# Sixteen attention units in a new order, and an output projection out of rounded operands

## The reference, cut to what matters

```
o_c = compressed attention, o_s = selected blocks, o_w = sliding window      # 8 heads, 2 KV heads, head_dim 64
g = sigmoid(gl)
o_att = g[0] * o_c + g[1] * o_s + g[2] * o_w
mixed = concat([rmsnorm(o_lru, out_norm_lru), rmsnorm(o_att, out_norm_att)]) @ w_out
x = x + gt1 * mixed
```

## Time and profile before

| | us |
|---|---|
| median of three runs | 1754.97 |
| lowest, highest | 1753.71, 1760.32 |
| profiled execution, own time | 1750.48 |
| its span | 1748.8 |
| TensorE busy in the span | 1681.2 (96%) |
| VectorE busy | 1298.6 (74%) |
| ScalarE busy | 668.0 (38%) |
| GpSimd busy | 375.2 (21%) |

### The profile page before, as it was taken

One profiled execution on the slowest core, in us unless ns is written; L12 is line 12 of the kernel. 1 busy time (PEld: TensorE's weight loads), 2 busy tenths in 40 slices (PEclk: granted clock), 3 DMA queues, 4 the chain that ended last, 5 costly groups with the idle time before them and its releaser, 6 DMA issues.

```text
span 1748.8 us, 30656 instructions
## 1 busy us (share of the span) xinstructions
PE 1681.2 (96%) x11657; PEld 1567.4 (90%) x11657; DVE 1298.6 (74%) x2673; ACT 668.0 (38%) x1048; POOL 375.2 (21%) x369
## 2 busy tenths in 40 slices
PE   7999997789899999999999999999999999999997
PEld 5699965458799999999899999999999999999997
DVE  0445546751677799998999999948878787878786
ACT  1336524740422233444344444443333333333332
POOL 3211000000000002111454445422322222222220
PEclk9999986999899999999999999999999999999998
DMA  9787676000623147766899999999999999999991
GB/s 342 271 272 273 213 213 242 1 1 1 242 82 99 63 134 275 245 225 210 297 384 383 388 371 390 385 373 387 402 373 337 347 343 345 346 342 351 339 319 63
DMA packets 178038, 466.43 MB, mean 267 GB/s; under 512 B 20399, under 2 KB 92335, under 8 KB 176251
## 3 DMA queue, kind: packets, MB, share of 16 engines
q1 hardware_dynamic: 130298, 289.53, 46.7%
q0 software_dynamic: 44880, 172.82, 26.9%
q10 hardware_dynamic: 2736, 2.49, 0.5%
HBM read 408.21 MB, written 63.37 MB: 270 GB/s over the span
## 4 chain that ended last, share of the span: by engine, by line
PE 86%; DVE 7%; DMA 3%; ACT 2%; issue 1%; ACTq 1%; POOL 0%; DVEq 0%
PE ps L1119 31%; PE ps L1005 26%; PE ps L735 10%; PE ps L957 3%; PE ps L1098 2%; PE ps L640 2%; ACT arena L1162 2%; PE ps L613 1%; PE ps L933 1%; PE ps L925 1%; DVE arena L1697 1%; DVE ul L1832 1%; PE ps L862 1%; PE ps L1014 1%; DMA gw<-stage 1%
## 5 line engine op out<-in xcount | busy, mean ns | idle before, releaser
L1832 DVE TENSOR_TENSOR ul<-raw,uh 128x1024 fp32r<-128x1024 f32 x256 | 311.5, 1222 | 109.8 <-ACT uh L1162 108.2
L1005 PE MATMUL ps<-hh,uh 128*128 128x392 f32 x1024 | 357.4, 349 | 1.6 <-DVE ul L1832 1.6
L1005 PE MATMUL ps<-hl,uh 128*128 128x392 f32 x1024 | 349.0, 341 | 0.0
L1005 PE MATMUL ps<-hh,ul 128*128 128x392 f32 x1024 | 348.6, 340 | 0.0
L1119 PE MATMUL ps<-ah,ul 128*128 128x392 f32 x1000 | 341.9, 342 | 0.0
L1119 PE MATMUL ps<-al,uh 128*128 128x392 f32 x1000 | 341.0, 341 | 0.0
L1119 PE MATMUL ps<-ah,uh 128*128 128x392 f32 x1000 | 339.7, 340 | 0.6 <-DVE al L2055 0.6
L1162 ACT ACTIVATE uh<-raw 128x1024 fp32r<-128x1024 f32 x256 | 270.0, 1056 | 103.3 <-PE ps L1119 89.5
L545 POOL DMA_INDIRECT xT<-in_u,gidx x128 | 177.5, 1387 | 545.1 <-DVE zg L1880 330.2
L545 POOL DMA_INDIRECT xT<-in_v,gidx x128 | 138.1, 1079 | 377.0 <-DVE vacc L2069 359.3
L1162 ACT ACTIVATE zbuf<-ps 128x392 f32<-128x392 f32 x128 | 63.7, 498 | 359.9 <-PE ps L1005 359.8
(11 more groups left out here) (371 smaller groups left out, 2279.4 us busy)
## 6 DMA issues: line engine op xcount, KB each, us to landing
raw<-in_uT SPq DMA_DIRECT2D x128, 512.0 KB, 5.6
raw<-in_v SPq DMA_DIRECT2D x128, 512.0 KB, 6.4
gw<-stage POOLq DMA_DIRECT2D x28, 896.0 KB, 10.8
gr<-gw SPq DMA_DIRECT2D x32, 784.0 KB, 8.3
zs<-zbuf SPq DMA_DIRECT2D x124, 196.0 KB, 5.7
zin<-zs SPq DMA_DIRECT2D x124, 196.0 KB, 5.9
arena<-in_ada_w SPq DMA_DIRECT2D x32, 512.0 KB, 4.3
arena<-in_w_in SPq DMA_DIRECT2D x18, 512.0 KB, 6.3
```

Source lines behind the costliest of these rows:

```text
L1005: last = mm(ps[:, bank, 0:DN], w[x][:, k * P:(k + 1) * P], m[:, k, G0:TOK], start=(k == 0 and x == 0 and m is hh), stop=(k == KD - 1 and x ...
L1832: tt(ul[:, i % 4, :], raw[:, i % 4, :], uh[:, i % 4, :].bitcast(F32), SUB).then_inc(S["lo_done"], 1)
```

## The change

In the attention, the three loops get a new order:

- TensorE: `scores(u + 1)`, then, block by block, the transpositions of unit u (`turn`) and one block of products of unit u - 1 (`apply`). `ptb` has eight blocks in place of four, so two units' turned blocks can stand side by side.
- ScalarE: the exponentials of u + 1 before the scalings of u.
- VectorE: `ttr(u + 1)` before `scale(u)`; the outputs of a query block are moved one unit later.

The output projection is made from rounded operands: ScalarE makes the high parts of the weights (`high_wo`, one per chunk of 128 columns) and of the input (`m_hi`), VectorE the low parts in the place of the originals (`low_wo`, `m_lo`), and TensorE makes three products in place of one fp32 product. Squares of the attention half go to another place, and the counts of some semaphores shift (`WQ_0`, `HQ_0`).

```diff
@@ buffers
+        with nc.sbuf_tensor("m_lo", [P, KD, TOK], F32R) as m_lo:
...
+        with (nc.sbuf_tensor("m_gap", [P, 9360], F32), nc.sbuf_tensor("m_hi", [P, KD, TOK], F32R) as m_hi,
...
-        ptb = at(13520, 4, GRP * P)
+        ptb = at(13520, 8, GRP * P)
@@ TensorE
+            first_turn = [sum(i + 1 for i, _, _ in units[:u]) for u in range(16)]
+
+            def turn(u, kb):
+                if kb == 0:
+                    pe.wait_ge(S["u_p"], GRP * (u + 1))
+                n = first_turn[u] + kb
+                if n >= 2:
+                    pe.wait_ge(S["u_tdone"], n - 1)
+                for r in range(GRP):
+                    last = pe.transpose(ps[:, 4 + n % 2, r * P:(r + 1) * P],
+                                        pbuf[:, (u % 2) * GRP + r, kb * P:(kb + 1) * P], ident[:, :])
+                last.then_inc(S["u_t"], 1)
...
+            def apply(u, kb):
                 i, br, w = units[u]
-                pe.wait_ge(S["u_p"], GRP * (u + 1))
...
+                if kb == 0 and u % 4 == 0 and i >= 2:
+                    pe.wait_ge(S["o_done"], i - 1)
+                if kb == 0 and br == 0:
+                    cached(i, w)
+                pe.wait_ge(S["u_tdone"], first_turn[u] + kb + 1)
+                pt = ptb[:, (u % 2) * 4 + kb, :].rearrange("p (r g q) -> p r g q", g=2, q=P)
+                for g in range(2):
+                    last = mm(ps[half(g), 6 + i % 2, 2 * w * P:2 * (w + 1) * P], vn[:, br * 4 + kb, half(g)], pt[:, :, g, :],
+                              start=False, stop=(br == 1 and kb == i))
+                if kb == i:
+                    last.then_inc(S["u_pv"], 1)
 
             pe.wait_ge(S["pc_tdone"], 4)
...
+            for u in range(17):
+                if u < 15:
+                    scores(u + 1)
+                for kb in range(4):
+                    if u < 16 and kb <= units[u][0]:
+                        turn(u, kb)
+                    if u >= 1 and kb <= units[u - 1][0]:
+                        apply(u - 1, kb)
 
             def project(c, ks):
+                pe.wait_ge(S["wql_done"], WO_0 + c + 1)
+                w = (wo_hi(c), wo_lo[:, :, c * P:(c + 1) * P])
                 for k in ks:
-                    for h in range(2):
-                        last = mm(ps[:, 2 + 2 * (c % 3) + h, 0:HALF], wout[:, k, c * P:(c + 1) * P],
-                                  zT[:, k, h * HALF:(h + 1) * HALF], start=(k == 0), stop=(k == KD - 1))
+                    if c == 0:
+                        pe.wait_ge(S["hl_ready"], MX_0 + max(1, k - 2))
+                    for x, m in ((0, m_hi), (0, m_lo), (1, m_hi)):
+                        for h in range(2):
+                            last = mm(ps[:, 2 + 2 * (c % 3) + h, 0:HALF], w[x][:, k, :], m[:, k, h * HALF:(h + 1) * HALF],
+                                      start=(k == 0 and x == 0 and m is m_hi), stop=(k == KD - 1 and x == 1))
...
-            pe.wait_ge(S["mix_ready"], 1)
@@ ScalarE
-            for u, (i, br, g) in enumerate(units):
-                nk = (i + 1) * P
+            def exps(u):
+                nk = (units[u][0] + 1) * P
                 act.wait_ge(S["u_max"], u + 1)
                 for r in range(GRP):
                     fn(pbuf[:, (u % 2) * GRP + r, 0:nk], pbuf[:, (u % 2) * GRP + r, 0:nk], ACT.Exp,
                        bias=pst(u, 1)[:, r:r + 1], accum_out=pst(u, 2)[:, r:r + 1]).then_inc(S["u_exp"], 1)
+            exps(0)
+            for u in range(16):
+                if u < 15:
+                    exps(u + 1)
+                nk = (units[u][0] + 1) * P
                 act.wait_ge(S["u_exp"], GRP * (u + 1))
                 act.wait_ge(S["u_rs"], u + 1)
                 for r in range(GRP):
                     fn(pbuf[:, (u % 2) * GRP + r, 0:nk], pbuf[:, (u % 2) * GRP + r, 0:nk], ACT.Copy,
                        scale=pst(u, 3)[:, r:r + 1]).then_inc(S["u_p"], 1)
+
+            def high_wo(c):
+                fn(wo_hi(c), wout[:, :, c * P:(c + 1) * P], ACT.Copy).then_inc(S["rounded"], 1)
+            act.wait_ge(S["wout_loaded"], 16)
+            high_wo(0)
+            act.wait_ge(S["lru_dve"], 6)
+            act.wait_ge(S["u_pv"], 12)
+            fn(m_hi[:, 0:4, :], zT[:, 0:4, :], ACT.Copy).then_inc(S["hh_ready"], 1)
+            high_wo(1)
+            high_wo(2)
             act.wait_ge(S["o_done"], 4)
-            fn(hT[:, 0:4, :], zT[:, 4:8, :], ACT.Square).then_inc(S["mix_sq"], 1)
+            fn(x1sq[:, 0:4, :], zT[:, 4:8, :], ACT.Square).then_inc(S["mix_sq"], 1)
             root(3, roots)
+            for c in range(4):
+                act.wait_ge(S["mix_ready"], c + 1)
+                fn(m_hi[:, 4 + c, :], zT[:, 4 + c, :], ACT.Copy).then_inc(S["hh_ready"], 1)
+            high_wo(3)
             for k in range(KD):
                 act.wait_ge(S["proj_ready"], k + 1)
                 fn(x1sq[:, k, :], xT[:, k, :], ACT.Square).then_inc(S["chunk_sq"], 1)
+                if k + 4 < KD:
+                    high_wo(k + 4)
@@ VectorE
+            def low_wo(c):
+                dve.wait_ge(S["rounded"], WO_0 + c + 1)
+                cols = slice(c * P, (c + 1) * P)
+                tt(wo_lo[:, :, cols], wout[:, :, cols], wo_hi(c).bitcast(F32), SUB).then_inc(S["wql_done"], 1)
...
-                    if u >= 1:
-                        dve.wait_ge(S["u_pv"], u)
-                    cp(ptb[:, kb, :], ps[:, 4 + (tcount[0] - 1) % 2, 0:512]).then_inc(S["u_tdone"], 1)
+                    if u >= 2:
+                        dve.wait_ge(S["u_pv"], u - 1)
+                    cp(ptb[:, (u % 2) * 4 + kb, :], ps[:, 4 + (tcount[0] - 1) % 2, 0:512]).then_inc(S["u_tdone"], 1)
...
-            for i in range(4):
-                for q in range(4):
-                    u = 4 * i + q
-                    scale(u)
-                    if u < 15:
-                        ttr(u + 1)
-                    evac(u)
+            def out_moved(i):
                 dve.wait_ge(S["u_pv"], 4 * i + 4)
                 link(cp(zT[:, 4:8, i * P:(i + 1) * P], ps[:, 6 + i % 2, 0:512].rearrange("p (r q) -> p r q", q=P)))
                 dve.sem_inc(S["o_done"], 1)
+            for u in range(16):
+                if u < 15:
+                    ttr(u + 1)
+                scale(u)
+                evac(u)
+                if u and u % 4 == 0:
+                    out_moved(u // 4 - 1)
+            low_wo(0)
+            dve.wait_ge(S["hh_ready"], MX_0 + 1)
+            tt(m_lo[:, 0:4, :], zT[:, 0:4, :], m_hi[:, 0:4, :].bitcast(F32), SUB).then_inc(S["hl_ready"], 1)
+            out_moved(3)
+            for c in (1, 2):
+                low_wo(c)
...
+            for c in range(4):
+                stt(zT[:, 4 + c, 0:SEQ], zT[:, 4 + c, 0:SEQ], par[:, NAG + c:NAG + c + 1], ps[:, 1, :], MUL, MUL).then_inc(S["mix_ready"], 1)
+            for c in range(4):
+                dve.wait_ge(S["hh_ready"], MX_0 + 2 + c)
+                tt(m_lo[:, 4 + c, :], zT[:, 4 + c, :], m_hi[:, 4 + c, :].bitcast(F32), SUB).then_inc(S["hl_ready"], 1)
+            low_wo(3)
...
                 dve.sem_inc(S["proj_ready"], 1)
+                if c + 4 < KD:
+                    low_wo(c + 4)
```

More of the change, by code:

```diff
@@ L67 @@
 KEPT = 4
+WO_0, MX_0 = ZC - 1, KD
+WQ_0, HQ_0 = WO_0 + KD, MX_0 + 5
 ADA_HEAD, ADA_ALL = 4, 36
@@ L125, in build @@
               nc.sbuf_tensor("wl0", [P, KD, P], F32R) as wl0):
+            pass
+        with nc.sbuf_tensor("m_lo", [P, KD, TOK], F32R) as m_lo:
+            pass
+        with (nc.sbuf_tensor("m_gap", [P, 9360], F32), nc.sbuf_tensor("m_hi", [P, KD, TOK], F32R) as m_hi,
+              nc.sbuf_tensor("wo_gap", [P, 17680 - 13520], F32), nc.sbuf_tensor("wo_pages0", [P, 8, 256], F32R) as wo_pages0,
+              nc.sbuf_tensor("wo_pages1", [P, 8, 256], F32R) as wo_pages1, nc.sbuf_tensor("wo_pages2", [P, 8, 256], F32R) as wo_pages2,
+              nc.sbuf_tensor("wo_pages3", [P, 8, 256], F32R) as wo_pages3, nc.sbuf_tensor("wo_lo", [P, KD, D], F32R) as wo_lo):
             pass
@@ L302, in heads, with wo_hi @@
             return [(2 * w + j // 2, j % 2) for j in range(GRP)]
+        def wo_hi(c):
+            return (wo_pages0, wo_pages1, wo_pages2, wo_pages3)[c % 4][:, :, P:2 * P]
         def load_w1(engine, c, s):
@@ L912, in _ @@
                 turn_cached(i)
-            tcount = [0]
-            def apply(u):
-                i, br, w = units[u]
-                pe.wait_ge(S["u_p"], GRP * (u + 1))
[L919 to L935, removed]
@@ L937, in _ @@
-            pe.wait_ge(S["pc_tdone"], 4)
-            for i in range(4):
-                for q in range(4):
-                    u = 4 * i + q
-                    if u < 15:
[L942 to L950, removed]
+            first_turn = [sum(i + 1 for i, _, _ in units[:u]) for u in range(16)]
@@ new lines, in cached @@
+            def cached(i, w):
+                cols = slice(2 * w * P, 2 * (w + 1) * P)
+                for g in range(2):
+                    mm(ps[half(g), 6 + i % 2, cols], vc[0:NCMP_P, 8, half(g)],
```

(26 more changed lines are left out.)

## The result

| | before | changed |
|---|---|---|
| median, us | 1755.26 (4 runs) | 1846.40 (4 runs) |
| lowest, highest | 1753.71, 1760.32 | 1843.09, 1850.21 |
| profiled execution, own time | 1750.48 | 1847.32 |
| its span | 1748.8 | 1845.6 |

The changed kernel takes 1.0516 times as long (95% interval 1.0483 to 1.0549): 91 us more. It was forecast slower, at 1831 in a range of 1798 to 1857.

What follows compares the result with a forecast made beforehand. TensorE's chain was taken to bound the kernel (86% of waits), with attention bound by hand-overs and the projection by columns. Ring +59, clock +28, projection -11 gave +76 on 1754.97: 1831 us, range 1798 to 1857.

Steps and rivals of the forecast that it cites:

- The ring: Attention: scores, sums, exponentials of u+1, normalisation, transposes of u, then scores of u+2 run strictly one after another; +59 us.
- the other side, faster: Rival, attention: scores run a turn ahead of the transposes, the ring stays open and ScalarE bounds; 1721 us, chance 0.03.
- The ring's size at the high clock: Attention: the ring's added time if the clock stays high, +59 us; a 512-key unit 13.2 us against 7.71.
- 40 blocks at 0.43 + 0.47: 36.0: Attention, TensorE's part of the ring: 40 blocks, each 0.43 us for a transposition and 0.47 for a product.
- The interpolated starts: Attention: scores start to exponentials start, units 1 to 15, middle sizes interpolated between 2.12 and 4.04 us; 47 us in all.
- The clock: Attention: TensorE's pauses drop its clock, units 0 to 7 all low, later bursts' first two pairs low; +28 us.
- clock rival: Either of two: the attention's clock stays high (1803 us, chance 0.16) or stays low throughout (1854 us, chance 0.20).
- The projection: Output projection: 384 records of rounded operands, 46.2 us in place of 58.2, with +1 of stall; -11 us.
- the seams: Projection: two new waits at the seam, for the strip sums' root and chunk 4's low part; +1 us, bounds 0 and 5.
- The low parts ahead of the outputs' move: Attention's end: VectorE makes low parts of first weights (1.22 us) and four input chunks (estimated 2.5) before moving outputs.
- a projection that waits for low parts: Listed sign, in the profile after, that the prediction would be wrong; no size given.
- The cover for the other low parts: Projection: VectorE needs 4.4 us a chunk within TensorE's 5.8, so low parts cost nothing; uncovered, four chunks 1.2 late each.

Runs made afterwards that it cites:

- e2: The kernel before with only ScalarE's swap, exponentials of u+1 ahead of the normalisation of u: 1836.3 us, ratio 1.0456.
- e6: The kernel before with TensorE's interleaving and VectorE's sums ahead of the scale, ScalarE in its old order, fp32 projection: 1820.0 us, ratio 1.0367.
- e5: The changed kernel with TensorE's pause in each turn filled by transpositions of the identity that no result uses: 1813.7 us, ratio 1.0321 against the kernel before.
- e8: The kernel before with the rounded projection alone, its first rounding moved into ScalarE's and VectorE's pauses in the last units: 1746.4 us, ratio 0.9934.
- e3: The kernel before with TensorE's interleaving alone, outputs moved one unit later, ScalarE and VectorE in their old order: 1765.2 us, ratio 1.0052.
- e9: The kernel before with TensorE making all transposes of u ahead of all products of u-1, other engines in old order, fp32 projection: 1766.3 us, ratio 1.0073.
- e12: Old attention and early rounded projection, plus ten filling transpositions of the identity ahead of each unit's wait: 1743.9 us, ratio 0.9932 against the kernel before.

## Why the prediction was right

**The ring** was the right mechanism: the list from 422.24 to 437.98 has its arrows in their order, and e2 and e6 each close a ring with a part of the change. Its rivals fell: the other side, faster, needed scores ahead of transposes, and none came.

**The ring's size at the high clock** is the term that was too small: 59 forecast, 70 measured (172.2 in e5, less 3.8 of fillers in the way, less 98.5). The step is "40 blocks at 0.43 + 0.47: 36.0". These were prices of runs of like records, 0.86 for two transposed blocks and 1.87 for four products. Alternating, a pair takes 1.17 (e5), 0.27 more, 10.8 for 40, and that is the difference. The price of a single block was in sight: 0.58 from 290.94 to the next scores (291.52), behind the 0.65 of the earlier trace rows, and it is what one record group costs when another kind follows. The interpolated starts held: scores start to exponentials start, units 1 to 15, adds up to 47.4 in e5, for 47. What is left is small on either side and partly cancels: hand-overs below the forecast, and the low spells of e5 above it.

**The clock**: +28 forecast for bursts that begin low and rise; e5 took 29.4 off, 33 with the fillers' 3.8 taken out. What the lower level adds to a pair was right, 0.93 (2.10 from 431.93 to 434.02, less 1.17) for 0.94, although both levels were 0.27 too cheap. The fall was complete in units 0 to 7, as taken. The count behind that was too low: in the bursts of units 9 to 11 every pair was low or nearly so, where two of three had been taken, and in the last four bursts two to two and a half. Against the high price the eight later bursts lost some 20 us, an estimate from the starts of their groups, for 15 forecast. Neither clock rival held: it didn't stay high (0.65), and it did rise within the bursts of 512 keys (436.00 to 440.00 at 0.95).

**The projection**: -11 forecast, -8.2 in the changed kernel, -9.7 in e5 and e8. The pitch of a run was exact, 0.24 for two records, but a whole chunk gains less than its 48 records. The chain of waits of the profile after has it, in start, length, group, and behind it a chunk before, to be held against the one at 412.94 in the earlier trace rows:

```profile
509.58 5.95 PE ps L980 x48
515.89 5.95 PE ps L980 x48
```

```profile
420.52 7.28 PE L957 MATMUL ps<-arena 128*128 128x260 f32 x32
```

With the sums between them, chunks stand 6.31 apart after and 7.58 before: 1.27 less, where the forecast's prices give 1.5. The 7.28 counted the last record to its end, 0.07 past the start of the sums, and after the change the records on either side of the sums take 0.1 more. Over eight chunks that is 2 us. Another 1.5 was missed at the start, where the clock was low after the wait for the low parts: a pair of records every 0.43 in place of 0.24. Against that, the seams cost less than the 1 us that had been counted for them.

The low parts ahead of the outputs' move, counted with the attention at 3.7, took 3.4 (483.11 to 486.48). They do hold up the first product, by 2.66, and "a projection that waits for low parts" had been named as a sign of being wrong; the wait was in the sum, not in the list of signs. The cover for the other low parts held: no product after the seam waits for one.

In all 59 + 28 - 11 = 76 was forecast and 103.1 - 8.2 = 95 measured in the profile, or 91 in the medians: 11 of the difference are the ring, 5 the clock and 3 the projection. All three errors point the same way. One sign shows them: the outputs were to be moved near 468 and were moved at 487.2, of which 2.9 is the later start. The time still lies in the range because the range was wide enough for either clock.

## What to carry to other kernels

Before an order is changed on several engines, write the new order of each as a list and follow one unit round all of them: if the next unit's first step sits behind this unit's last on every engine, the engines take turns. Moving the next unit's work ahead helps only if the step that feeds it was moved ahead on the other engines as well, by the same number of units. A ring with long pauses pays a second time through TensorE's clock; here that was some 33 us of 103, and one run with idle transpositions in the pauses showed it.

## What the runs showed of the hardware

- Short groups of unlike matmuls took longer than their run price: a transposed block 0.43 in a run and 0.58 before a product, a product block 0.47 in a run and 0.58 before a transposition, at the high clock; 1.05 each at the low one, where a transposed block in a run took 0.90 (before, 351.44). It cost time only inside the ring: in e3, without one, a unit took 7.30 all the same, against 7.28 in e9. Whether the kind or the semaphore wait ahead of each group makes it isn't shown.
- Small pauses can cost much: in e9, with TensorE busy 86.6 of 109 us, the granted clock was 0.78, and ten idle transpositions a unit (632 records in place of 472) raised it to 0.98 and took 12.5 us off. The kernel before had 0.88 with 77.4 of 98.5 us busy. Why e9's pauses pull it lower than those of before isn't settled here.
- Filling pauses isn't always worth it: in e12 the clock rose by 0.05 and the stage got 2.3 longer, and in e5 the last unit's fillers held its transposes up by 3.0 us.
